# Expert stage: one ScalarE function for x * sigmoid(x), the activation in three parts, the weights' parts in another order

## The reference, cut to what matters

```
for e in range(N_EXPERTS):            # 16
    a = silu(hf @ w_e_gate[e]) * (hf @ w_e_up[e])      # gate, up: 1024 x 512
    y = y + combine[:, e:e + 1] * (a @ w_e_down[e])    # down: 512 x 1024
```

## Time and profile before

| | |
|---|---|
| median of three runs | 1394.6 us (1394.38 to 1396.15) |
| the profiled execution | 1396.64 us |
| its span, first to last instruction | 1394.8 us |
| TensorE busy | 1316.3 us, 94% of the span |
| VectorE busy | 779.7 us, 56% |
| ScalarE busy | 555.1 us, 40% |
| experts' stage | from 838.84 to about 1323 us |

### The profile page before, as it was taken

One profiled execution on the slowest core, in us unless ns is written; L12 is line 12 of the kernel. 1 busy time (PEld: TensorE's weight loads), 2 busy tenths in 40 slices (PEclk: granted clock), 3 DMA queues, 4 the chain that ended last, 5 costly groups with the idle time before them and its releaser, 6 DMA issues.

```text
span 1394.8 us, 19837 instructions
## 1 busy us (share of the span) xinstructions
PE 1316.3 (94%) x7309; PEld 1017.4 (73%) x7310; DVE 779.7 (56%) x1014; ACT 555.1 (40%) x734; POOL 318.5 (23%) x449
## 2 busy tenths in 40 slices
PE   4999999999999999999999989999999999999984
PEld 2666678998787666666778777887777888887752
DVE  5734222324402267666799864558887242458648
ACT  0432022322212255555412143457776242457522
POOL 0133210003100257666166510000000000000053
PEclk9999999999999999999999999999999999999997
DMA  9854320102211342110433359669999151649764
GB/s 334 312 182 124 121 68 1 62 1 76 68 46 42 86 160 62 31 42 21 181 103 102 136 200 394 236 240 350 385 391 363 67 219 60 241 173 379 268 231 168
DMA packets 138776, 234.54 MB, mean 168 GB/s; under 512 B 57328, under 2 KB 58936, under 8 KB 138712
## 3 DMA queue, kind: packets, MB, share of 16 engines
q1 hardware_dynamic: 128440, 196.41, 39.9%
q0 software_dynamic: 6496, 23.60, 4.9%
q10 hardware_dynamic: 3776, 13.67, 2.4%
HBM read 197.96 MB, written 35.68 MB: 168 GB/s over the span
## 4 chain that ended last, share of the span: by engine, by line
PE 70%; POOL 7%; issue 6%; DVE 6%; ACT 5%; DMA 3%; SPq 1%; ACTq 1%; POOLq 0%; DVEq 0%
PE psum L831 65%; POOL arena L2098 5%; ACT high L1519 2%; DMA arena<-in_w_ada_mix 2%; PE psum L1243 1%; PE psum L1058 1%; DVE arena L2037 1%; DVE arena L2036 1%; PE psum L938 1%; ACT a_high L1551 1%; DVE arena L2029 1%; PE psum L1249 1%; DVE arena L2028 1%; PE psum L882 1%; PE psum L1152 0%
## 5 line engine op out<-in xcount | busy, mean ns | idle before, releaser
L831 PE MATMUL psum<-arena 128*64 128x128 f32 (+8 forms) x1396 | 165.9, 368 | 24.0 <-DMA arena<-in_w_ada_mix 15.1
L831 PE MATMUL psum<-win_high,x_low 128*128 128x512 f32 (+1 forms) x432 | 168.5, 390 | 0.0
L831 PE MATMUL psum<-high,h_high 128*128 128x512 f32 x416 | 163.8, 394 | 2.5 <-DVE h_low L1984 2.5
L831 PE MATMUL psum<-win_high,x_high 128*128 128x512 f32 (+1 forms) x416 | 166.2, 399 | 0.0
L831 PE MATMUL psum<-win_low,x_high 128*128 128x512 f32 (+1 forms) x416 | 162.3, 390 | 0.0
L831 PE MATMUL psum<-high,h_low 128*128 128x512 f32 x416 | 162.2, 390 | 0.0
L831 PEld LDWEIGHTS psum<-arena 128*64 128x64 f32 (+4 forms) x1396 | 83.2, 143 | 100.6 <-issue 72.7
L1840 DVE TENSOR_TENSOR_SCAN arena<-arena,psum 128x512 f32<-128x512 f32 (+3 forms) x112 | 108.2, 1003 | 19.8 <-ACT arena L1475 19.5
L1979 DVE TENSOR_TENSOR low_odd<-raw_odd,high 128x2048 fp32r<-128x2048 f32 x48 | 107.8, 2288 | 14.0 <-ACT high L1519 14.0
L1979 DVE TENSOR_TENSOR low_even<-raw_even,high 128x2048 fp32r<-128x2048 f32 x48 | 107.7, 2287 | 10.9 <-ACT high L1519 10.8
L2155 POOL COPY smalls<-smalls 128x1 int32 x26 | 4.8, 183 | 417.6 <-PE psum L1243 412.8
(11 more groups left out here) (260 smaller groups left out, 2417.2 us busy)
## 6 DMA issues: line engine op xcount, KB each, us to landing
raw_even<-in_w_e_gate SPq DMA_DIRECT2D x8, 2048.0 KB, 10.9
raw_even<-in_w_e_up SPq DMA_DIRECT2D x8, 2048.0 KB, 16.8
raw_even<-in_w_e_down SPq DMA_DIRECT2D x8, 2048.0 KB, 14.7
raw_odd<-in_w_e_gate SPq DMA_DIRECT2D x8, 2048.0 KB, 10.2
raw_odd<-in_w_e_up SPq DMA_DIRECT2D x8, 2048.0 KB, 16.4
raw_odd<-in_w_e_down SPq DMA_DIRECT2D x8, 2048.0 KB, 15.0
win<-in_w_in SPq DMA_DIRECT2D x7, 2048.0 KB, 7.9
expert_rows<-arena ACTq DMA_DIRECT2D x26, 512.0 KB, 6.5
```

What stands on the lines that cost most here:

```text
L831: pe_last[0] = nc.tensor.matmul(*x, **y)
```

## The change

Six things are done. ScalarE's sigmoid and VectorE's multiplication by bank 0 become one ScalarE function, Silu, and VectorE multiplies its output with bank 1. The activation is worked on in three parts of one, one and two tiles of 128 columns (`act_parts`), where there were two halves; the third part's transposes go to bank 0, the first two to banks 6 and 7. ScalarE makes the next expert's weight parts 0 and 1 behind Silu and 2 and 3 later, where it was 0 and then 1, 2, 3. VectorE's low part 5 moves from behind the loop to the first block of the expert that it belongs to, and low part 0 of the next expert stands ahead of all multiplies of the block. The small transpose and `s_edone` go; the waits on it become waits on `s_yp`, the count of blocks whose down products are done. One Silu of a single column is issued at the end of routing.

```diff
@@ -338,7 +338,6 @@
         s_e = [[sem(f"expert_{w}_in{i}") for w in ("gate", "up", "down")] for i in range(2)]
-        s_edone = sem("expert_done")
         s_idx, s_hg, s_htr, s_hL = sem("index_ready"), sem("rows_gathered"), sem("rows_turned2"), sem("block_h_low")
@@ -360,6 +359,8 @@
         pieces = ((0, 4, 3), (4, 8, 11), (8, 9, 16))
+        act_parts = ((0, 1, 6), (1, 2, 7), (2, 4, 0))
+        N_ACT = len(act_parts)
@@ -556,7 +557,7 @@
         yb = view(r_b + 16384, D)
-        an = view(r_b + 17408, 2, 256)
+        an = view(r_b + 17408, 512)
         zero_rows = view(r_m + EXPERT_W, D)
@@ -616,6 +617,7 @@
         idc = rtiny(1, dt=I32)
+        table_warm = rtiny(1)
@@ -803,10 +805,11 @@
                         if i == 2:
-                            sp.wait_ge(s_edone, 2 * ee + k - 1)
+                            sp.wait_ge(s_yp, end)
                         src = w[0, bass.ds(2 * ee + k, 1)].rearrange("e (k p) n -> p (e k) n", p=P)
                         sp.dma_start(raw_w[k][i], src).then_inc(s_e[k][i], 16)
-            sp.wait_ge(s_edone, EXPERTS - 1)
+            end = sp.value_load(table[0:1, EXPERTS - 1:EXPERTS], min_val=1, max_val=MAX_BLOCKS - 1)
+            sp.wait_ge(s_yp, end)
             for t in range(TILES):
@@ -1243,30 +1246,29 @@
                         last.then_inc(s_htr, 1)
-                        for half in range(2):
-                            pe.wait_ge(s_a, 2 * b + half + 1)
-                            for f in range(2):
-                                last = nc.tensor.transpose(bank(6 + half)[:, f * P:(f + 1) * P],
-                                                           an[:, half, f * P:(f + 1) * P], ident)
+                        for i, (f0, f1, at) in enumerate(act_parts):
+                            pe.wait_ge(s_a, N_ACT * b + i + 1)
+                            for f in range(f0, f1):
+                                last = nc.tensor.transpose(bank(at)[:, (f - f0) * P:(f - f0 + 1) * P],
+                                                           an[:, f * P:(f + 1) * P], ident)
                             last.then_inc(s_at, 1)
...
                         for f in range(FC):
-                            if f % 2 == 0:
-                                pe.wait_ge(s_aH, 2 * b + f // 2 + 1)
+                            part = [i for i, (f0, f1, _) in enumerate(act_parts) if f0 == f]
+                            if part:
+                                pe.wait_ge(s_aH, N_ACT * b + part[0] + 1)
                             for hh in range(2):
...
                                 mm(psum[2][:, hh, :], a_high[:, f, :], low_w[k][2][:, f, cols], start=False, stop=False)
-                            if f % 2 == 0:
-                                pe.wait_ge(s_aL, 2 * b + f // 2 + 1)
+                            if part:
+                                pe.wait_ge(s_aL, N_ACT * b + part[0] + 1)
                             for hh in range(2):
...
                         last.then_inc(s_yp, 1)
-                    nc.tensor.transpose(bank(7)[0:64, 0:64], ident[0:64, 0:64], ident[0:64, 0:64]).then_inc(s_edone, 1)
@@ -1509,6 +1511,7 @@
             A(dd, dd, ACT.Exp).then_inc(s_rt2, 1)
+            A(table_warm, mhalf[:, 0:1], ACT.Silu)
@@ -1542,19 +1545,19 @@
                         act.wait_ge(s_gu, 2 * b + 1)
-                        A(sg, bank(0), ACT.Sigmoid).then_inc(s_sg, 1)
+                        A(sg, bank(0), ACT.Silu).then_inc(s_sg, 1)
                         if follows:
                             with act.If(b + 1 == end):
-                                high_parts(nxt, (0,), loads)
-                        for half in range(2):
-                            act.wait_ge(s_at, 2 * b + half + 1)
-                            A(a_high[:, 2 * half:2 * half + 2], bank(6 + half)[:, 0:256].rearrange(
-                                "p (f q) -> p f q", f=2), ACT.Copy).then_inc(s_aH, 1)
+                                high_parts(nxt, (0, 1), loads)
+                        for i, (f0, f1, at) in enumerate(act_parts):
+                            act.wait_ge(s_at, N_ACT * b + i + 1)
+                            A(a_high[:, f0:f1], bank(at)[:, 0:(f1 - f0) * P].rearrange(
+                                "p (f q) -> p f q", q=P), ACT.Copy).then_inc(s_aH, 1)
                         act.wait_ge(s_htr, b + 2)
...
                             with act.If(b + 1 == end):
-                                high_parts(nxt, (1, 2, 3), loads)
+                                high_parts(nxt, (2, 3), loads)
                         act.wait_ge(s_yp, b + 1)
@@ -1568,7 +1571,6 @@
-            act.wait_ge(s_edone, EXPERTS)
             for t in range(TILES + 2):
@@ -1982,7 +1984,7 @@
             TT(h_low_2, psum[1][:], h_high_f, ALU.subtract).then_inc(s_hL, 1)
-            low_parts(0, (3, 4, 5), 0)
+            low_parts(0, (3, 4), 0)
@@ -1992,26 +1994,27 @@
                     with dve.Fori(first, end) as b:
-                        dve.wait_ge(s_sg, b + 1)
-                        TT(an.rearrange("p a c -> p (a c)"), sg, bank(0), ALU.mult).then_inc(s_g1, 1)
+                        with dve.If(b == first):
+                            low_parts(k, (5,), before - 6)
                         if follows:
...
                                 low_parts(nxt, (0,), before)
-                        dve.wait_ge(s_g1, b + 1)
+                        dve.wait_ge(s_sg, b + 1)
                         dve.wait_ge(s_gu, 2 * b + 2)
-                        for half in range(2):
-                            TT(an[:, half], an[:, half], bank(1)[:, half * 256:half * 256 + 256], ALU.mult).then_inc(s_a, 1)
-                        for half in range(2):
-                            dve.wait_ge(s_aH, 2 * b + half + 1)
-                            TT(a_low[:, 2 * half:2 * half + 2], bank(6 + half)[:, 0:256].rearrange(
-                                "p (f q) -> p f q", f=2), a_high_f[:, 2 * half:2 * half + 2], ALU.subtract).then_inc(s_aL, 1)
+                        for f0, f1, _ in act_parts:
+                            fs = slice(f0 * P, f1 * P)
+                            TT(an[:, fs], sg[:, fs], bank(1)[:, fs], ALU.mult).then_inc(s_a, 1)
+                        for i, (f0, f1, at) in enumerate(act_parts):
+                            dve.wait_ge(s_aH, N_ACT * b + i + 1)
+                            TT(a_low[:, f0:f1], bank(at)[:, 0:(f1 - f0) * P].rearrange(
+                                "p (f q) -> p f q", q=P), a_high_f[:, f0:f1], ALU.subtract).then_inc(s_aL, 1)
                         dve.wait_ge(s_hH, b + 2)
...
                     if follows:
-                        low_parts(nxt, (4, 5), before)
+                        low_parts(nxt, (4,), before)
@@ -2159,7 +2162,7 @@
             pool.sem_inc(s_go, 1)
-            pool.wait_ge(s_edone, EXPERTS)
+            pool.wait_ge(s_yp, total)
             pool.sem_inc(s_go, 1)
```

## The result

The changed kernel takes 1379.96 us (median of four runs, 1378.37 to 1385.27); the kernel before, with the runs made beside it, 1395.38. The ratio is 0.9896, its 95% interval 0.987 to 0.9922. The profiled executions give the same: spans 1394.8 and 1379.6 us.

The account below looks back on a forecast made before the run. The prediction took TensorE, with its holes in the experts' stage, as the bound. Savings of 5.5 + 1.5 + 3.6 = 10.6 us from 1394.6 gave 1384.0 us, with an 8-in-10 range of 1381.0 to 1389.0.

Parts of the forecast that it names:

- Hole one: TensorE's 0.51 us wait per block for ScalarE's first `a_high` copy; three parts save 0.21 per block, 5.5 us.
- Cover: Before the down products: three multiplies take at most 1.1 us; third copies have six products, some 1.4 us, ahead.
- the free waits: The two added waits on TensorE find their semaphores set and cost nothing; at 0.05 us each, 2.6 us.
- Hole three: 3.6 us lost, mostly in one-block experts, through a ScalarE and VectorE chain; Silu, no table load and reordering regain it.
- The walk after the first copy: One-block chain retimed from the first `a_high` copy at period 18.32: VectorE free 0.6 us early, ScalarE's part 1 2.2.
- Hole two: Change of expert costs 0.36 us, 15 times; removing the small transpose saves 0.10 each, 1.5 us, bounds 0 and 2.6.
- The transfers: One-block experts become DMA-bound if 385 GB/s is the ceiling: 1385.8 us; 20% together with Hole three staying.
- the three signs: Wrong if the wait before down products keeps 0.5 us, one-block periods stay above 18.6, or ScalarE's part 0 awaits loads.
- VectorE late: Low parts and conditions ahead of VectorE's multiplies delay TensorE in one-block experts: 1397.4 us; slower or nothing 5%.

Follow-up runs that it names:

- turns interleaved: The changed kernel with the first activation tile's transpose moved behind the fifth of the next block's eight row transposes: 1376.68 us, ratio 0.9849.

## Why the prediction was right or wrong

**Hole one, three parts: right.** 0.21 per block was forecast, 0.214 measured, from the first activation turn to the first down product 0.73 us instead of 0.95 (0.74 forecast). A 128-column copy takes 0.28 where a 256-column one takes 0.38, as worked out. Cover and the free waits are as said.

**Hole three, Silu and order: right in size and chain.** 3.6 us forecast, 3.6 measured by Silu alone. The walk after the first copy holds to 0.25 us. VectorE has 0.37 us to spare where 0.6 were worked out, because the period came out at 18.04 and not at 18.32. What the prediction didn't see is the division: the table load is 2.0 of it, Silu with it all 3.6, and the order pays only at the shorter period, 1.9 us.

**Hole two, the small transpose: wrong, and this is the step that failed.** "Its slot is 987.64 - 987.47 = 0.17 us ... The register loads that follow it stay, and some of the slot is theirs. Bounds 0 and 2.6; I take 0.10, 1.5 us." The upper bound was none. The prediction had itself measured the whole cost of a change of expert, 18.63 - 18.27 = 0.36, and put it down to the change, leaving the transpose a part of its slot. (The pair it read gives the least; others in that trace lie up to 0.45 apart, 18.68 against 18.23.) The runs show that all of it is the transpose: without it a change costs nothing. The kernel before with Silu (462.3) and the changed kernel with two halves (456.3) differ in the transpose and the order of parts: 6.0 us for 16 changes, 0.38 each, against 1.5; in the changed kernel's pace it is 6.8, and where the difference of 0.8 lies is open. The price lies on both sides of the slot: the 0.09 before it, the 0.17 of the slot, where a full transpose takes 0.03, and 0.16 in the gate and up products behind, of which 0.10 in the first; behind a full transpose these are 0.12 slower as well. With the terms as they came one after the other the sum is 3.6 (Silu) + 6.0 (transpose, order) + 5.4 (three parts) = 15.0, the 15.0 measured; it has to close, since each is a difference of two kernels in a row.

**The terms are not independent.** Alone, the small transpose gives 2.6 us and three parts 2.9, since ScalarE's chain paces nine periods; only with Silu do both gain wherever they stand. Adding the three terms up, as the prediction did, holds only because all three were made together.

**Rivals and signs.** The transfers: the mechanism is there, and the slack was enough. The 385 GB/s were no ceiling. The window that answers to the earlier trace rows:

```profile
945.00:1057.00 112.00, 111.45 (x523) 91.91 (x522) 101.31 (x81) 86.83 (x75) 6.92 (x12) 1.00 1.03 397
```

and landings of the gate weights issued at 957.54 and at 1047.77, where the earlier trace rows has 10.6:

```profile
raw_odd<-in_w_e_gate SPq DMA_DIRECT2D x1, 2048.0 KB, 11.3
...
raw_even<-in_w_e_gate SPq DMA_DIRECT2D x1, 2048.0 KB, 14.4
```

At a period of 18.04 each load lands later than the one before, by 3.1 us over five experts; the queue does grow. At the end of the run ScalarE's part 0 waits 0.28 us for a load (1042.98). That is one of the three signs by which the prediction called itself wrong; it came once, and no period is longer for it. The other two, a wait of 0.5 us and periods above 18.6, did not come. 397 GB/s is above the 358 that the Trainium skill's page "DMA: Bandwidth & Descriptors", section "Where 436 GB/s comes from", gives for HBM transfers of one core; the measurement decides. With turns interleaved the rival comes true. VectorE late: no, its wait is for TensorE.

## What to carry to other kernels

When a hole at a seam is measured (here 0.36 us per change of expert) and the change takes away one instruction of that seam, the bound of the gain is the whole hole, not the slot between two starts: look whether the next weight load lies ahead of its product or right on it. A tiny instruction on TensorE used as a signal can cost nearly two steps of a product (0.42 against 0.23 us) if it uses 64 rows among neighbours of 128; the semaphore on the last product costs nothing that can be seen. And walk the chain of every engine again at the new period: an order that was worth nothing at 18.63 mattered at 18.04, and transfers that were hidden there held up the stage at 17.75.

## What the hardware showed beyond that

An fp32 transpose with 64 rows between 128-row products costs 0.44 us with 64 or 128 columns (10.9 and 11.1 us over 25), one with 128 rows 0.16 (4.1 us with 64 columns, over 25; 2.6 us for 16 full ones). Branches and register loads between two experts cost TensorE nothing when the instructions around them are of one shape: the step across them is the 0.23 us of all others. With DMA engines always busy, this mix of 2 MB weight loads, gathers and stores gave 397 GB/s over 112 us, and 399 where the stage waited for it.
